# Samples' contexts in fp32 from unsplit probabilities, the loop over page groups written out, prompt items through three PSUM banks

## The reference

```python
c_all = concat([cache_kv_latent[pt].reshape(past, KV_LORA), ci])      # 4096 + 8 rows of 256
k = mla_keys(c_all, kr_all, w_uk, g_kn_nope, g_kn_rope)               # keys of 8 heads, normalised
s = einsum('qhd,khd->hqk', qi, k) * SCALE
p = softmax(where(mask[None], s, -inf), axis=-1)
ctx = einsum('hqk,kr->qhr', p, c_all)                                 # "context": 64 rows (8 heads x 8 tokens) of 256
out = einsum('qhr,rhv->qhv', ctx, w_uv)
```

## Time and profile before

| | |
|---|---|
| Time, median of 3 runs | 2210.32 us (2210.22 to 2210.33) |
| The profiled execution's own time | 2214.44 us |
| Its span in the trace | 2212.4 us |
| PE busy | 2102.2 us, 95% |
| DVE, ACT, POOL busy | 53%, 37%, 17% |
| Mean granted TensorE clock | 0.972 of full |

### The profile page before, as it was taken

One profiled execution on the slowest core, in us unless ns is written; L12 is line 12 of the kernel. 1 busy time (PEld: TensorE's weight loads), 2 busy tenths in 40 slices (PEclk: granted clock), 3 DMA queues, 4 the chain that ended last, 5 costly groups with the idle time before them and its releaser, 6 DMA issues. The chain is left out here.

```text
span 2212.4 us, 36454 instructions
## 1 busy us (share of the span) xinstructions
PE 2102.2 (95%) x12673; PEld 1930.5 (87%) x12673; DVE 1177.6 (53%) x2358; ACT 813.5 (37%) x1585; POOL 379.5 (17%) x436
## 2 busy tenths in 40 slices
PE   6998999969988999999999979999999999999998
PEld 5887999958887999999999968898989998989897
DVE  4764311146765777667767744445454445454444
ACT  4552111145553566556656633322221112221111
POOL 1110000023441145355535501000000000000000
PEclk8999999989998999999999988999999999999999
DMA  4233222134322312222222107021111111111102
GB/s 151 84 87 82 59 79 79 65 99 133 111 79 62 89 36 63 74 61 66 63 68 65 42 29 261 1 77 39 58 38 57 38 38 38 57 38 57 38 19 86
DMA packets 146211, 152.90 MB, mean 69 GB/s; under 512 B 50694, under 2 KB 122102, under 8 KB 145021
## 3 DMA queue, kind: packets, MB, share of 16 engines
q1 hardware_dynamic: 140325, 128.28, 19.6%
q0 software_dynamic: 5728, 22.65, 3.3%
HBM read 124.77 MB, written 25.97 MB: 68 GB/s over the span
## 5 line engine op out<-in xcount | busy, mean ns | idle before, releaser
L104 PE MATMUL ps<-mh,f_w1h 128*128 128x384 f32 (+1 forms) x768 | 250.6, 326 | 0.0
L106 PE MATMUL ps<-mh,f_w1l 128*128 128x384 f32 (+1 forms) x768 | 250.5, 326 | 0.0
L105 PE MATMUL ps<-ml,f_w1h 128*128 128x384 f32 (+1 forms) x768 | 250.3, 326 | 0.0
L1346 ACT ACTIVATE sq<-ps 128x512 f32<-128x512 f32 x256 | 153.0, 598 | 219.6 <-PE ps L106 219.6
L1898 ACT ACTIVATE tail_room<-ps 128x384 f32<-128x384 f32 (+1 forms) x96 | 45.5, 474 | 502.1 <-PE ps L106 502.1
L1943 DVE TENSOR_TENSOR t_m<-t_m,ps 128x512 f32<-128x512 f32 x256 | 171.5, 684 | 107.1 <-PE ps L106 107.1
L105 PE MATMUL ps<-f_late_l,f_late_h 128*128 128x512 f32 x512 | 199.9, 390 | 0.0
L106 PE MATMUL ps<-f_late_h,f_late_l 128*128 128x512 f32 x512 | 199.8, 390 | 0.0
L104 PE MATMUL ps<-f_late_h 128*128 128x512 f32 x512 | 199.3, 389 | 0.0
L1923 DVE TENSOR_TENSOR tail_room<-tail_room 128x384 f32<-128x384 f32 (+1 forms) x96 | 51.5, 536 | 253.8 <-ACT tail_room L1898 253.8
L104 PE MATMUL ps<-wq,cTh 128*128 128x320 f32 x512 | 173.2, 338 | 6.5 <-DVE g_attn_b L1410 6.5
(11 more groups left out here) (348 smaller groups left out, 5067.2 us busy)
## 6 DMA issues: line engine op xcount, KB each, us to landing
f_raw<-in_w_ff SPq DMA_DIRECT2D x32, 1024.0 KB, 5.2
c_ring<-in_cache_kv_latent SPq DMA_DIRECT2D x192, 128.0 KB, 2.0
m_raw<-in_w_in SPq DMA_DIRECT2D x20, 512.0 KB, 4.0
gated<-gate POOLq DMA_DIRECT2D x8, 1088.0 KB, 5.2
pa_gm<-gated SPq DMA_DIRECT2D x16, 512.0 KB, 5.0
c_early<-in_cache_kv_latent SPq DMA_DIRECT2D x64, 128.0 KB, 2.0
fr_x<-in_x_prompt SPq DMA_DIRECT2D x8, 512.0 KB, 3.5
mixed<-pa_mixed SPq DMA_DIRECT2D x16, 256.0 KB, 2.1
```

What stands on the lines that cost most here:

```text
L104: nc.tensor.matmul(out, lh, rh, start=first, stop=False)
L105: nc.tensor.matmul(out, lh, rl, start=False, stop=False)
L106: return nc.tensor.matmul(out, ll, rh, start=False, stop=last)
L1346: nc.scalar.activation(sq[:, j % 2, :].rearrange("p (a n) -> p a n", a=2), ps[:, kn_bank(j):kn_bank(j) + 2, 0:HALF], ACT.Square).then_inc( ...
```

## The change

There are three parts.

1. Contexts of the 7 sequences are fp32 matmuls of the probabilities as they are (64 columns) with the pages as they are, which have a 257th column of ones (L1248 after). The split parts, their copies and the fold are gone, on ACT, DVE, POOL and PE; the context is now first in a step, ahead of the transposes. The last sequence uses the same column and has no separate sums. ACT, DVE and POOL keep the rest of their work in its order, but for the division by the sum, which DVE now makes behind the scores of `page(0)`.
2. The loop is written out: 68 steps, with constants for the semaphore values and addresses. SP's loads too.
3. In prompt_attention the items go through banks 4, 5 and 6 (near the tile of 1040 keys through 5 and 6 alone), with four slots for the split probabilities; the product of an item comes three items later, that of a unit's first block four; and DVE gates behind the maximum of the item.

```diff
+    long_tiles = {s: n for n, s in enumerate(tile_at) if s is not None and seen[tile_of(s)] > 1024}
+    for n in range(N):
+        free = [5, 6] if any(m - 2 <= n <= m + 1 for m in long_tiles.values()) else [4, 5, 6]
+        bank_of.append(min(free, key=lambda bank: last_in(bank, n) if bank in bank_of else -1))
...
-                bank = 5 + n % 2
-                if n >= 2:
-                    pe.wait_ge(S["lo"], n - 1)
+                bank = bank_of[n]
+                if bank in bank_of[:n]:
+                    pe.wait_ge(S["lo"], last_in(bank, n) + 1)
+                over = [s for s in long_tiles if long_tiles[s] <= n]
+                if bank == 4 and over:
+                    pe.wait_ge(S["exp"], max(over) + 1)
...
-                j = n - 2
-                if j in block_no:
...
+                if n - 4 in firsts:
+                    product(n - 4)
+                if n - 3 in block_no and n - 3 not in firsts:
+                    product(n - 3)
...
-                with eng.Fori(1, NG // RING) as lap:
-                    for k in range(RING):
-                        emit(eng, k, lap * RING + k, lap, lambda x: True, True)
+                for g in range(NG + 4):
+                    emit(eng, g, lambda back, g=g: 0 <= g - back < NG)
...
-                def high(j):
-                    return nc.tensor.matmul(ps[:, 7, 0:KV + 2], prob_hl[:, gi * GP + j].rearrange("p s n -> p (s n)"),
-                                            ch[:, kc % 2, j, :], start=gi == 0 and j == 0, stop=gi == GS - 1 and j == GP - 1)
-                def low(j):
-                    nc.tensor.matmul(ps[0:HQ, 7, 0:KV + 2], prob_hl[:, gi * GP + j, 0, :], cl[:, kc % 2, j, :],
-                                     start=False, stop=False)
...
+                    last = nc.tensor.matmul(out, prob[:, b % 2, gi * GP + j, :], c_ring[x % RING][:, j, :],
+                                            start=gi == 0 and j == 0, stop=gi == GS - 1 and j == GP - 1)
...
+            if 0 <= g - LAG < NG - GS:
+                context(g - LAG)
...
-            if last_of(k, LAG + 1, valid):
-                pe.wait_ge(S["ctx_copied"], seq_of(lap, k, LAG + 1) + 1)
-                nc.tensor.matmul(ps[0:HQ, 7, 0:KV + 1], B["fold"][:], craw[:], start=True, stop=True).then_inc(S["folded"], 1)
...
-                nc.scalar.activation(ch[:, (k - LAG + 1) % 2, :, 0:KV], c_ring[(k - LAG + 1) % RING],
-                                     ACT.Copy).then_inc(S["c_hi"], 1)
...
-                nc.gpsimd.tensor_tensor(cl[:, (k - LAG + 1) % 2, :, 0:KV], c_ring[(k - LAG + 1) % RING],
-                                        f32(ch[:, (k - LAG + 1) % 2, :, 0:KV]), ALU.subtract).then_inc(S["c_lo"], 1)
```

More of the change, by code:

```diff
@@ new lines, in program, with last_of, pe_step, context @@
+                for g in range(NG + 4):
+                    emit(eng, g, lambda back, g=g: 0 <= g - back < NG)
+            return program
+        def last_of(g, back):
+            return 0 <= g - back < NG and (g - back) % GS == GS - 1
+        def pe_step(pe, g, valid):
+            k, p1 = g % RING, (g - 1) % 2
+            def context(x):
+                b, gi = x // GS, x % GS
+                if gi % 2 == 0:
+                    pe.wait_ge(S["exp"], b * NP + gi // 2 + 1)
+                if gi == 0 and b:
+                    pe.wait_ge(S["ctxn"], b)
+                out = ps[0:HQ, 7, 0:KV + 1]
+                if gi == GS - 1:
+                    nc.tensor.matmul(out, prob[:, b % 2, NPAGE, :], B["c_new"][:], start=False, stop=False)
@@ L1263, in context @@
                 for j in range(GP):
-                    low(j)
-                for j in range(gi == 0, GP):
-                    last = high(j)
+                    last = nc.tensor.matmul(out, prob[:, b % 2, gi * GP + j, :], c_ring[x % RING][:, j, :],
+                                            start=gi == 0 and j == 0, stop=gi == GS - 1 and j == GP - 1)
                 last.then_inc(S["ctx"], 1)
             def page(j):
-                if j == 0 and (k - 1) % GS == 0:
-                    pe.wait_ge(S["q"], seq_of(lap, k, 1) + 1)
+                x = g - 1
@@ L1308, in pe_step @@
             if valid(1):
+                page(0)
                 page(1)
-            first = (k - LAG) % GS == 0
-            if split_context(g, LAG, valid, loading) and not first:
-                context()
-            if maximum:
-                pe.wait_ge(S["lmax"], seq_of(lap, k, 3) + 1)
-                if loading:
+            if last_of(g, 3):
+                pe.wait_ge(S["lmax"], (g - 3) // GS + 1)
+                if valid(0):
                     pe.wait_ge(S["lo"], 2 * g + 2)
-                nc.tensor.matmul(ps[0:HQ, 0, 0:P], lmax[:, (k - 3) % RING // GS, :], C["ident"][:], start=True, stop=True
+                nc.tensor.matmul(ps[0:HQ, 0, 0:P], lmax[:, (g - 3) // GS % 2, :], C["ident"][:], start=True, stop=True
                                  ).then_inc(S["turned"], 1)
@@ L1637, in _ @@
             end = NSEQ - 1
-            for i in range(NP):
-                span = slice(parts[i].start, parts[i].stop + (i == NP - 1))
-                dve.wait_ge(S["exp"], end * NP + i + 1)
-                nc.vector.tensor_reduce(most[:, i, :], prob[:, 1, span, :].rearrange("p t n -> p n t"), AX.X, ALU.add
-                                        ).then_inc(S["sums"], 1)
             dve.wait_ge(S["end"], 1)
-            nc.vector.reciprocal(rden[:, end:end + 1], ps[0:HQ, 4, 0:1]).then_inc(S["rden"], 1)
+            nc.vector.reciprocal(rden[:, end:end + 1], ps[0:HQ, 3, KV:KV + 1]).then_inc(S["rden"], 1)
             dve.wait_ge(S["rden"], NSEQ)
```

403 lines of the change are left out of this document (162 added, 241 removed).

## The result

The changed kernel takes 2232.88 us (median of four runs, 2231.81 to 2234.21) against 2210.32 us: a ratio of 1.0098, interval 1.0086 to 1.011. The forecast was 2226.6 us in a range of 2212 to 2243. The sign, the bound and the size of the largest term were right; the whole was 6.3 us too low.

What follows compares the result with a forecast made beforehand. PE was taken to bound the sample steps and, as nearest bound, the prompt items. 54.1 - 2.0 - 5.0 - 4.4 - 7.3 - 6.9 - 12.2 = +16.3 us, added to the 2210.32 us median: 2226.6 us, range 2212 to 2243.

Steps and rivals of the forecast that it cites:

- Context blocks: Sample steps: four fp32 matmuls cost 1.97 us a block, 1.02 more than before; 53 blocks, +54.1 us.
- Cheap fp32: Rival in the context blocks: entering and leaving fp32 next to transposes costs nothing; 2216 us, chance 0.11.
- visible weight loads: Rival in the context blocks: fp32 weight loads are not hidden, 58 us more; 2285 us, chance 0.01.
- New row and fold: Sequences' contexts: the new tokens' row joins the fp32 block, -2.0 us; the fold goes, -5.0 us.
- PE's waits for L1410: Sample steps, once a sequence: PE's waits go as DVE divides after reading `page(0)`; -4.4 us.
- end of the samples: Last sequence: waits behind DVE's `cl`, the late last context and the sums over ones go; -6.9 us.
- The cover of `page(2)`: Sample steps: moving the block from before `page(2)` costs 0; rival that PE waits there: 10 us, 2237 us, chance 0.10.
- The loop: Sample steps: written out, the gaps at two jumps back and the half clock behind them go; -7.3 us.
- the 3.4 us of half clock: Loop: 1.7 us lost behind each of two jumps; prompt items: 3.4 us lost between 540.7 and 547.5 us.
- The prompt items: Prompt stage: one item more before PE needs the low part saves waits and half clock, 8.8 + 3.4; -12.2 us.
- the 8.8 us: Prompt stage: waits of PE's own rows for DVE, 4.7 + 3.2 + 0.9 us, counted as gain.
- The 4.7 us stay, since POOL's order doesn't change: Prompt stage: PE's stall without releaser, head 7's scores waiting for POOL's split of the keys, stays at 4.7 us.

Runs made afterwards that it cites:

- second trace of the loop: Trace of the kernel before with only the new prompt stage, its step loops kept; 2199.88 us, ratio 0.9958.
- the two old stages: The old prompt stage in the kernel before (2210.32 us) and in the changed kernel with the prompt function of before (2242.72 us, ratio 1.0148).

## Why the prediction was right, and where it was off

- **What bounds the steps.** Right: PE, 555.38 of 556 us busy, with 3.4 us of short waits behind that number. Taking POOL from 243 to 97 us and DVE from 393 to 339 gave no time back beyond the waits named.
- **Context blocks, +54.1.** Right in size and in build: 1.97 us a block as foreseen, 0.435 us a matmul and 0.23 us for the way in and out. Cheap fp32 and visible weight loads are refuted (0.216 us spacing, no gap). The way out is shared with the transposes, though; in the middle of the step the block costs 0.10 us more and lays a wait bare, 23 us in all. The forecast had no term for what the new place is worth, and it came out because it was priced from a matmul with a transpose behind it, which is also what stands behind the block in its new place.
- **New row and fold, PE's waits for L1410, end of the samples.** Together with the blocks 35.8 against 37.6 us measured. That is closer than it should be: 4.2 of the 37.6 us are the rope keys' transpose, so the terms as forecast measured 33.4. The end is -7.7 us in the trace against -6.9, but only 5.6 of it from the parts named.
- **The cover of `page(2)`, 0.** Right, with 0.5 us to spare.
- **The loop, -7.3.** The mechanism was right (both gaps go, straight code has none), the size too large: -4.9 us (-3.1 to -6.9). The step that failed is the one that took the 3.4 us of half clock from one execution, itself 4.1 us above the median, and added them to the median. In the second trace of the loop they are missing.
- **The prompt items, -12.2.** -11.3 us in the trace, -9.3 (-6.4 to -11.9) in the runs. The size is near, partly by luck, for it was not made of the rows that it was read in. PE's waits for DVE fell by 4.0 of the 8.8 us, those for POOL and without a releaser rose by 4.2, and the idle time of PE stayed; the gain is in its busy time. The 3.4 us of half clock hold for some executions only, and the two old stages with and without it differ by 1.7. "The 4.7 us stay, since POOL's order doesn't change" was wrong: the order doesn't change but the times do. In the changed kernel DVE's second gate operation takes 2.29 us instead of 0.69 beside POOL's split of the queries:

```profile
632.31 0.68 DVE L995 TENSOR_TENSOR pa_mixed<-ps,pa_gm 128x512 f32<-128x512 f32 x1
633.02 2.29 DVE L997 TENSOR_TENSOR pa_mixed<-pa_mixed,pa_gm 128x512 f32<-128x512 f32 x1
635.24 0.56 DVE L1024 TENSOR_TENSOR pa_pl<-ps,pa_ph 128x400 fp32r<-128x400 f32 x1
```
```profile
632.35 2.42 POOL L862 TENSOR_TENSOR pa_ql<-pa_q_raw,pa_qh 96x1024 fp32r<-96x1024 f32 x1 [1.95 <-ACT pa_qh L936]
...
638.58 2.37 POOL L862 TENSOR_TENSOR pa_kl<-pa_k_raw,pa_kh 96x1040 fp32r<-96x1040 f32 x1 [1.48 <-ACT pa_kh L936]
```

  The low part and the maximum come late, ACT's copy of the keys behind them too, and POOL's `pa_kl`, for which PE stands, ends at 640.95. From the start of the query split to the end of the key split it is 8.60 us, against 6.64 before: 1.96 us more, as the stall has 2.0 more. This chain is read from the traces; no run removes the overlap. Nor is the overlap new: in the kernel before, the same addition took 2.90 us in two other heads.
- **Not in the prediction at all.** The rope keys' transpose moved ahead of `page(0)`: 4.2 us. I read the context's move from the diff and passed over the one beside it.
- **The 6.3 us of miss.** 3.2 are in the trace (19.5 against 16.3): steps 1.9, prompt items 0.9, untouched stretches 1.2, end -0.8. In the steps the 3.4 us of the rope keys' transpose stand against 1.0 us more from the loop. The other 3.1 us come from adding a difference of profiled executions to a median: the execution of before was 4.1 us above its median, that of after 0.8 (their times differ by 19.2 us, their spans by 19.5). By the runs the parts are 37.6 - 9.3 - 4.9 = 23.4 us against 22.6 measured; loop and prompt were forecast 5.3 us too large a gain, and the terms for the contexts and the end 2.4 too dear, with 4.2 left out. The 1.2 us of the untouched stretches are not explained; they lie within the scatter of the runs.

The place of the gate was listed in the prediction as something against the prompt's gain ("the gate now waits on DVE for a product that PE issues in the same item"). Its other half, that the maximum was put ahead of it so that this wait harms nobody, was not: undoing it costs 20 us once the product comes three items behind.

## What to carry to other kernels

Where PE is the bound, price a change of number format by matmul instructions and by the switches between formats: four fp32 matmuls of 257 columns cost 1.97 us where eight float32r ones cost 0.95, and no relief of the other engines paid for that. Put what is in fp32 next to what is in fp32 already, and look at what the block covers where it stands. A pipeline's distance, its buffers and the order on the consumer's queue belong together: the three parts gave 9 to 13 us, and the longer distance without the third bank was 16 us slower than the old stage. Take small terms from several executions, not from one profile, when the clock wavers: both stretches at half clock that the forecast counted as gains were missing in another trace.

## What had not been expected of the hardware

- Leaving fp32 costs on the first float32r matmul, not on the block: 0.23 to 0.25 us to its neighbour instead of 0.15, the same behind one transpose and behind eight matmuls. Entering costs 0.09 us on the float32r matmul before a block of fp32 matmuls (0.21 us instead of 0.12), and nothing on the one before the transposes, though they are fp32 too (723.39 to 723.51 in the changed kernel, 0.12 us).
- The eight transposes behind a context block take 0.06 us more than behind a float32r matmul (0.85 against 0.79 us to `page(0)`, with the rope keys' transpose elsewhere).
- An addition with both inputs in SBUF took 0.69 us on DVE alone, 2.29 us beside POOL's split of the queries in the changed kernel, and up to 2.90 us in the kernel before. The one before it, with an input in PSUM, kept its 0.68 us. It goes the other way too: where the addition started first, by 0.03 us, POOL's split took 2.94 us instead of 2.41. The kernel before, in two heads:

```profile
509.44 0.69 DVE L989 TENSOR_TENSOR pa_mixed<-pa_mixed,pa_gm 128x512 f32<-128x512 f32 x1
509.47 2.94 POOL L855 TENSOR_TENSOR pa_ql<-pa_q_raw,pa_qh 96x1024 fp32r<-96x1024 f32 x1
...
534.99 2.41 POOL L855 TENSOR_TENSOR pa_ql<-pa_q_raw,pa_qh 96x1024 fp32r<-96x1024 f32 x1
535.04 2.90 DVE L989 TENSOR_TENSOR pa_mixed<-pa_mixed,pa_gm 128x512 f32<-128x512 f32 x1
```

  The Trainium skill (SBUF — State Buffer, section "SBUF: two separate sides") describes the port pair that DVE and GpSimd share as locked for a whole instruction by whichever starts first, the other fully blocked. The traces agree: in both orders the one that started first kept its time, and the late addition of the changed kernel ends at 635.31, 0.54 us after POOL's 2.42 us operation.
- A gap on PE was followed by half clock at some times and not at others: 1.83 and 2.05 us of gap at the loop's jumps were, in the trace of the kernel before, and 1.63 and 1.41 us at the same jumps were not, in the trace with the new prompt stage.
